# VectorE's step order and the share of GpSimd's low parts in a two-layer MLA, HGRN2 and PEER kernel

## The reference

```python
def _peer(h, w_q, sub_keys, u, v):
    def block(xt):
        q = (xt @ w_q).reshape(PEER_TBLOCK, PEER_HEADS, 2, PEER_HALF)
        s = jnp.einsum('thpd,hpnd->thpn', q, sub_keys).astype(jnp.float32)
        s1, i1 = lax.top_k(s[:, :, 0], PEER_TOPK)
        s2, i2 = lax.top_k(s[:, :, 1], PEER_TOPK)
        cand = s1[..., :, None] + s2[..., None, :]      # 16 x 16 per head
        cidx = i1[..., :, None] * PEER_NKEYS + i2[..., None, :]
        top, pos = lax.top_k(cand, PEER_TOPK)
        eidx = jnp.take_along_axis(cidx, pos, axis=-1)
        gates = jax.nn.softmax(top, axis=-1)
        act = jax.nn.gelu(jnp.einsum('td,thkd->thk', xt, u[eidx]))
        return jnp.einsum('thk,thkd->td', gates * act, v[eidx])
```

## Time and profile before

| | |
|---|---|
| median of 3 runs | 3225.55 us |
| the profiled execution | 3226.29 us |
| its span on the core | 3224.3 us |
| TensorE (matmul) busy | 3053.0 us, 95% |
| VectorE busy | 2380.4 us, 74% |
| ScalarE busy | 1190.6 us, 37% |
| GpSimd busy | 1058.1 us, 33% |
| granted TensorE clock, mean | 0.978 |
| DMA, mean | 248 GB/s |

### The profile page before, as it was taken

One profiled execution on the slowest core, in us unless ns is written; L12 is line 12 of the kernel. 1 busy time (PEld: TensorE's weight loads), 2 busy tenths in 40 slices (PEclk: granted clock), 3 DMA queues, 4 the chain that ended last, 5 costly groups with the idle time before them and its releaser, 6 DMA issues.

```text
span 3224.3 us, 44567 instructions
## 1 busy us (share of the span) xinstructions
PE 3053.0 (95%) x16468; PEld 2685.5 (83%) x16468; DVE 2380.4 (74%) x4512; ACT 1190.6 (37%) x1843; POOL 1058.1 (33%) x733
## 2 busy tenths in 40 slices
PE   7999997999999999999998989997999999999998
PEld 5658897998999888888787968997898898888887
DVE  5245898878877888888205876898788777888887
ACT  4343332343333333333433433332334333333333
POOL 3203463333333222222344423454333333222221
PEclk9899998999999999999998989998999999999999
DMA  3202366999999999998221002357999999999996
GB/s 131 71 14 98 102 197 227 299 341 316 338 328 396 365 355 353 353 356 312 85 92 53 2 27 100 114 179 274 319 317 343 320 340 407 357 355 353 353 352 240
DMA packets 345719, 800.86 MB, mean 248 GB/s; under 512 B 27936, under 2 KB 191776, under 8 KB 345248
## 3 DMA queue, kind: packets, MB, share of 16 engines
q1 hardware_dynamic: 271776, 529.55, 46.9%
q0 software_dynamic: 73728, 268.47, 23.1%
HBM read 695.15 MB, written 102.76 MB: 247 GB/s over the span
## 4 chain that ended last, share of the span: by engine, by line
PE 85%; DVE 11%; issue 2%; ACT 1%; DMA 0%; POOL 0%; SPq 0%; DVEq 0%; ACTq 0%
PE PS L1344 25%; PE PS L1346 24%; PE PS L1345 24%; PE PS L1505 3%; PE PS L1591 2%; PE PS L1566 2%; DVE arena L1009 1%; DVE arena L1045 1%; DVE arena L1041 1%; DVE arena L1006 1%; DVE arena L1311 1%; PE PS L1482 1%; DVE arena L1039 1%; PE PS L1443 1%; DVE arena L1012 1%
## 5 line engine op out<-in xcount | busy, mean ns | idle before, releaser
L1344 PE MATMUL PS<-x_hi,w_hi 128*128 128x384 f32 (+1 forms) x2616 | 927.5, 355 | 49.6 <-DVE w_lo L1121 34.8
L580 ACT ACTIVATE w_hi<-w_raw 128x1024 fp32r<-128x1024 f32 x609 | 642.8, 1056 | 755.6 <-PE PS L1346 750.8
L1346 PE MATMUL PS<-x_hi,w_lo 128*128 128x384 f32 (+1 forms) x2616 | 910.5, 348 | 0.0
L1345 PE MATMUL PS<-x_lo,w_hi 128*128 128x384 f32 (+1 forms) x2616 | 909.4, 348 | 0.0
L1121 DVE TENSOR_TENSOR w_lo<-w_raw,w_hi 128x1024 fp32r<-128x1024 f32 x456 | 558.0, 1224 | 380.4 <-ACT w_hi L580 359.6
L1344 PE MATMUL PS<-w_hi,x_hi 128*128 128x512 f32 x1744 | 682.4, 391 | 13.8 <-POOL w_lo L503 13.8
L1345 PE MATMUL PS<-w_lo,x_hi 128*128 128x512 f32 x1744 | 681.1, 391 | 0.0
L1346 PE MATMUL PS<-w_hi,x_lo 128*128 128x512 f32 x1744 | 680.8, 390 | 0.0
L514 POOL DMA_INDIRECT arena<-in_u_rows,arena x256 | 356.2, 1391 | 693.4 <-DVE arena L1128 595.6
L503 POOL TENSOR_TENSOR w_lo<-w_raw,w_hi 128x1024 fp32r<-128x1024 f32 x153 | 377.0, 2469 | 597.2 <-ACT w_hi L580 597.2
L1344 PEld LDWEIGHTS PS<-x_hi,w_hi 128*128 128x128 f32 x2616 | 494.1, 189 | 73.7 <-DVE w_lo L1121 35.4
(11 more groups left out here) (179 smaller groups left out, 2538.9 us busy)
## 6 DMA issues: line engine op xcount, KB each, us to landing
w_raw<-in_u_t SPq DMA_DIRECT2D x256, 512.0 KB
w_raw<-in_v_t SPq DMA_DIRECT2D x256, 512.0 KB
acts_dram<-arena SPq DMA_DIRECT2D x256, 192.0 KB
gates_dram<-arena SPq DMA_DIRECT2D x24, 2048.0 KB
arena<-gates_dram SPq DMA_DIRECT2D x64, 768.0 KB
arena<-acts_dram SPq DMA_DIRECT2D x256, 192.0 KB
w_raw<-in_hg_t SPq DMA_DIRECT2D x40, 512.0 KB
w_raw<-in_pq_t SPq DMA_DIRECT2D x32, 512.0 KB
```

The lines of the kernel that those rows point to most:

```text
L580: act.activation(w_hi[:, slot, :], w_raw[:, slot, :], ACT.Copy).then_inc(hi_ready, 1)
L1344: pe.matmul(ps, wh, xh, start=start, stop=False)
L1345: pe.matmul(ps, wh, xl, start=False, stop=False)
L1346: return pe.matmul(ps, wl, xh, start=False, stop=stop)
```

## The change

Inside a step of VectorE's loop the low part of tile s + 3 moves from the first place to the last. GpSimd makes the low parts of tiles 0 to 35 of u where it made those of 0 to 27, so VectorE's loop begins at step 33 where it began at 25, and its first low part is that of tile 36. The softmax of the gates moves from step 28 to 34, TensorE's `route_rows` from tile 32 to 38, `routes` from step 33 to 39. The quads lie over tiles 41 to 117 (77 tiles) where they lay over 36 to 115 (80), and the dots over steps 33 to 127 (95) where they lay over 25 to 127 (103). Both layers are changed alike.

```diff
-FIRST_DVE_LOW = 28
-ROUTES_AT = 32
-FIRST_QUAD, END_QUAD = 36, 116
+FIRST_DVE_LOW = 36
+ROUTES_AT = 38
+FIRST_QUAD, END_QUAD = 41, 118
...
                 for s in range(FIRST_DVE_LOW - RING + 1, 2 * NKEYS):
-                    if s + RING - 1 < 2 * NKEYS:
-                        low(bu + s + RING - 1)
                     if s == ROUTES_AT - 4:
                         gates()
...
                     if s >= NKEYS:
                         far_add(s - NKEYS)
+                    if s + RING - 1 < 2 * NKEYS:
+                        low(bu + s + RING - 1)
```

## The result

The median falls from 3226.56 us (four runs) to 3133.52 us (four runs, 3129.78 to 3135.27): a ratio of 0.9711 with a 95% interval of 0.9699 to 0.9723. The forecast was 3182, with 3173 to 3204 as its range. The change brought 93 us where 44 were expected.

What follows compares the result with a forecast made beforehand. TensorE's matmuls fill 95% of the span, so only its stops or low clock can yield time. 3226.3 us less 46.1 for two stops, plus 1.4 and 2 in charges, less 2 for fewer switches, gave 3182, range 3173 to 3204.

Steps and rivals of the forecast that it cites:

- The u side after the stops: u tiles behind the first quad: reordering costs nothing, VectorE's 26% idle time covers 0.2 us more work a tile.
- fewer switches: Three fewer u tiles with quads save switching between two kinds of matmul: 1 us per layer, bounds 0 and 1.5.
- The two stops: TensorE's stops at u tiles 28 and 36, with the low clock: 24.3 and 21.8 us lost, 46.1 to win.
- GpSimd's low parts against the routes: Eight more GpSimd low parts slow VectorE's routing by 10.6 us, ending near 522; bounds 511.6 and 528.5.
- rival (a): GpSimd's low parts delay the routes by the full 17 us, to 528.5: 6.7 us per layer, 3195; chance 0.14.
- The first octet: VectorE ends the first quad's octet at 548.8, TensorE arrives at 550.4; charged 0.7 us per layer, bounds 0 and 4.1.
- The v side: v tiles: low part starts 2.5 us later, activation margin shrinks from 12.1 to 8.9 us, no steady cost.
- rival (c): v side bound by activations' landing, from 8.8 us up: 3453 if in all tiles; chance 0.05, 0.01 at no change.
- From u to v: Last gate store two tiles later delays v's first loads and products: charged 1 us per layer, bounds 0 and 8.
- The sum: Whole kernel: 3226.3 - 46.1 + 2 x 0.7 + 2 x 1 - 2 x 1 = 3181.6, stated as 3182 us.
- The chances: Whole kernel: as forecast (3174 to 3190) 0.64; faster by over 0.2% 0.91, within 0.05, slower 0.04.
- The low end: Range's lower limit, 3173 us: no charges, 3 us for fewer quad tiles and 3 for what could not be seen.

Runs made afterwards that it cites:

- 116: The changed kernel with the quads ending at END_QUAD 116 instead of 118: 3120.36 us and again 3121.88 us, ratios 0.9673 and 0.9671.
- 114: The changed kernel with the quads ending at END_QUAD 114 instead of 118: 3120.39 us, ratio 0.9673.
- The order alone: The kernel before with only the new step order (low part last), tile and step constants as before: 3162.05 us, ratio 0.9797.
- the constants alone: The kernel before with only the new constants (FIRST_DVE_LOW 36, ROUTES_AT 38, quads 41 to 118), order as before: 3204.12 us, ratio 0.9932.
- the dots kernel: The kernel before with only the dots moved ahead of the low part, octets and products still behind it: 3234.49 us, ratio 1.0009.

## Why the prediction was wrong

**The u side after the stops: the step that failed.** It said "Low part and work only rotate" and "No cost", and took VectorE's mean idle time as cover. It asked only whether the new order would cost something there; in fact the old one did, and the term that was put at nothing was a gain of 57 us. In the old order the octet stood behind the low part of tile s + 3, which waits for ScalarE; low part and octet together end about when TensorE comes to the quads of tile s + 1, mostly after. I worked this chain out for the first octet, where the stop was large enough to be seen, and not for the other 47, of which 35 in each layer were late with 0.68 us of idleness each. The two layers lost 28.7 and 28.8 us there (519.7 - 466.7 - 24.3 and 517.3 - 466.7 - 21.8), 57.5 in all. Of these 48 us are idleness before L1505 (52.7 less 2.4 for each first octet); the rest goes with it, as in the example above. Two rows could have told it: the 52.7 us of idleness before L1505, which I read as the cost of a switch between kinds of matmul ("I take 1 us per layer for fewer switches"), and the sum of the tiles. I compared tiles and ideal up to tile 36 and found 24.3 us. The same sum up to tile 127 gives 53.0.

**The two stops.** Right. Both are gone with their low clock, 46.1 us; TensorE's clock is at 1.00 through that stretch.

**GpSimd's low parts against the routes.** Right: the routes' end was put near 522 and came at 521.87 + 0.29 = 522.2, 10.5 us later than before, for eight low parts. That it came within 0.2 us is luck in part: five of eight was a choice between bounds of 0 and 17 us. The lock that the Trainium skill describes ("SBUF — State Buffer", "Who interferes with whom") agrees with the traces in kind: in the kernel before, a product of 128x2048 with two inputs (L1041) takes 1.23 us in the fourth route, without GpSimd's low parts. One in the second route starts at 439.98, while GpSimd makes a low part until 442.19, and takes 3.30 us. The searches (L1009) take 0.29 us in both routes, so the price for all eight low parts was too high, and rival (a) did not come. Two inputs are not the only case: a `TENSOR_SCALAR` with one input (L1028) took 2.75 us in the second route and 0.23 in the fourth.

**The first octet.** Right: forecast 548.8, measured 549.3; TensorE came to it at 550.5, the Gelu of tile 40. No charge of 0.7 was due.

**The v side.** The shift was right: in one round of the changed kernel, ScalarE and VectorE,

```profile
1154.07 1.06 ACT L580 ACTIVATE w_hi<-w_raw 128x1024 fp32r<-128x1024 f32 x1 [2.60 <-PE PS L1346]
...
1157.71 1.22 DVE L1121 TENSOR_TENSOR w_lo<-w_raw,w_hi 128x1024 fp32r<-128x1024 f32 x1
```

the low part starts 3.64 us after the high part (forecast 1206.6 - 1203.0 = 3.6), and the round takes 4.08 us. Of VectorE's waits from 1060 to 1450 us, the one for activations:

```profile
DVE arena L1155 <- DMA arena<-acts_dram: 16.8, 9, 2.7
```

That is a wait that did not exist in that stretch before. So the margin of rival (c) was as thin as worked out: a median landing of 7.2 us against 8.9 allowed, with some landings beyond it. TensorE did not feel it.

**From u to v.** 1 us per layer was charged, 0.7 and 0.6 measured (396.6 and 396.5 against 395.9). Right in size and, as 116 and 114 show, in cause. The order alone, with the quads ending where they did, has 395.9 in both layers, and the constants alone 396.1 and 396.3: by itself neither costs more than a part of it.

**The sum.** 52.9 and 50.0 us in the two layers' PEER (53.6 - 0.7, 50.6 - 0.6) make 102.9; the recurrence took 8.8 us more in the profiled execution, which leaves 94.1 for a span that is 94.3 shorter.

**The chances.** "Faster" at 0.91 was right. The range failed because no rival allowed for a gain on the u side, and the one bound that did went to 1.5 us per layer, for fewer switches. The low end was made of charges taken away and 3 us for the unseen.

## What to carry to other kernels

An engine works its queue in order, so an operation that waits delays all that stands behind it. Put what is needed sooner ahead of the wait, even if the wait is short, and compare the end of each such operation with the moment its reader comes to it. A mean idle share is no cover. And hold the whole stretch against its ideal (tiles times the time of one) before pricing single stops: what is missing there and has no name is often a small wait at each turn, which the profile may file under "issue".

## What the runs showed of the hardware

**The recurrence takes one of two times.** Between the PEER layers, from the high part of the last tile but three ahead of the recurrence to the first one behind it, all twelve traces take either 201.3 to 201.6 us or 210.2 to 210.3. Near its start TensorE pauses for 5.2 us, until 1737.81 in the kernel before and until 1685.00 in the changed one. After the pause the granted clock is 0.50 in both. The kernel before, first, and the changed one, second (columns as in the earlier trace rows), right behind the pause and from 18 us behind it:

```profile
1738.00:1750.00 12.00, 10.34 (x47) 9.71 (x47) 7.36 (x12) 6.86 (x16) 5.42 (x5) 0.50 0.07 29
...
1756.00:1776.00 20.00, 20.00 (x183) 20.00 (x181) 17.70 (x34) 8.08 (x21) 10.06 (x10) 1.00 0.01 2
```

```profile
1685.00:1697.00 12.00, 10.34 (x46) 9.70 (x46) 7.25 (x12) 7.04 (x16) 5.42 (x5) 0.50 0.09 34
...
1703.00:1723.00 20.00, 20.00 (x128) 20.00 (x127) 8.67 (x20) 5.61 (x15) 6.93 (x7) 0.68 0.00 1
```

The clock is at half for 13.7 us in the one and for 30.7 in the other, the later part of it with TensorE busy without a gap. It is 13.7 in all six traces with the shorter recurrence and 30.7 in all six with the longer. Seventeen more microseconds at half speed are 8.5 us of lost work, about the whole difference. The change does not touch this stretch: a second trace of the changed kernel has 201.3 us, and one of the dots kernel, with the old constants, 210.2. A difference under 9 us between two such kernels has to be looked for in the stretches, not in one total. The two kinds also differ in when the clock falls: 3.3 to 4.0 us after the start of the last high part ahead of the recurrence in the shorter ones, 4.9 to 5.1 in the longer. What decides between them was not tried.

**GpSimd's gathers grow longer beside VectorE.** The issue of a gather of a v row took 1005 ns in the mean before (the page's part 5) and takes 1744 after:

```profile
L514 POOL DMA_INDIRECT arena<-in_v_t,arena x256 | 446.6, 1744 | 594.2 <-DVE resid L1144 547.0
```

`far_add` and the low part, both with two inputs, now follow one another without a gap, and the issue falls into them. Before, the issue began in the gap between the two (1207.75 us, with `far_add` of the earlier trace rows ending at 1207.48). No time is seen to be lost by it: after the change GpSimd still stands idle for 547 us waiting for `far_add` to give back its buffers.
